# Moving the big on-chip tiles of a two-block transformer kernel to addresses that are multiples of 1024 bytes

## The chip, the cores and the metric

The kernel runs on one core of one Trainium2 chip. A core has a matmul engine (TensorE, PE in the profile; its weight loads are shown apart as PEld), VectorE (DVE), ScalarE (ACT), GpSimd (POOL) and SyncE (SP), which here issues nearly all DMAs. They share the on-chip memory SBUF, 128 partitions wide, in which a tile has one start address that is the same in all partitions. The metric is the device time of one execution in microseconds; lower is better.

## What is computed

The input is 256 tokens of 1024 features, float32, batch 1. Two transformer blocks of different kind follow each other:

```
x = first_block(x, mem, ...)          # one layer
#   h += [dilated attention | gated linear recurrence] @ w_out
#   h += cross attention to mem (q from h; k, v from rmsnorm(mem))
#   h += relu(rmsnorm(h) @ w_mlp_in)^2 @ w_mlp_out ; final rmsnorm
x = second_block(x, ...)              # two layers
#   z = rmsnorm(x) @ w_in ; MLA, FNet, differential attention, HGRN2 scan
#   x += (sum of gated branches) @ w_out
#   x += (silu(g) * u) @ w_down ,  [g | u] = rmsnorm(x) @ w_gate_up
```

All arithmetic is float32, and nearly all of the work is multiplying 256 tokens by some 190 MB of weights that are each used once.

## The kernel before

**Pieces.** The weights are packed on the host into 192 pieces of 128 partitions x 2048 floats (1 MB, 8192 bytes in a partition; 54 for the first block, 69 for each layer of the second). SyncE loads them in order into `ring`, a buffer of three pieces (`load_piece`, L993 to L1000).

**Split products.** A float32 matmul at full precision is replaced by three faster ones on split operands: w = w_hi + w_lo and x = x_hi + x_lo, and the product is x_hi w_hi + x_lo w_hi + x_hi w_lo. For each piece ScalarE writes `w_hi` (two instructions of 128x1024, L1125), VectorE writes `w_lo` = ring - w_hi (one of 128x2048, L1625), and TensorE then runs 48 matmuls of 256 columns (2 halves x 3 passes x 8 blocks of the contraction): `gemm` (L530 ff.), every one issued through `mm` (L508). `w_hi` and `w_lo` hold two pieces each, so that the next piece is split while TensorE works on this one. I call the 48 matmuls of a piece a job.

**Moving and stationary.** A matmul streams one operand (moving) past another that was loaded into the array before (stationary). In the "feat" form (L547) x moves and the weight is stationary: the profile names it `bank<-x_hi,w_hi`, moving operand first. In the "tok" form the weight moves and x is stationary: `bank<-w_hi,x_hi`. The product of the cross attention's keys and values uses `mem_hi` and `mem_lo` in the place of x. In the three down projections the weight moves in runs of 512 columns against the stationary hidden activations (`bank<-w_hi,hid_hi`). So a 256-column matmul reads 1024 contiguous bytes in each partition as moving operand and 512 bytes as stationary operand, whose place within a row of 1024 bytes is the operand's start (first half) or 512 bytes further (second half).

**Where tiles lie.** `sb` (L162) gives out SBUF in the order of the calls, L168 to L187. Four large tiles, `hid_hi`, `hid_lo`, `mem_hi` and `mem_lo`, are placed at offsets inside the arena `W` (L180 to L184), from which all scratch tensors are cut by number. Nothing in the program's order depends on addresses: steps, waits and semaphores are the same whatever they are.

The start addresses in the built program, and what is left after dividing by 1024:

| tile | before: address (mod 1024) | changed: address (mod 1024) |
|---|---|---|
| ring | 16512 (128) | 17408 (0) |
| w_hi | 41088 (128) | 41984 (0) |
| w_lo | 57472 (128) | 58368 (0) |
| const | 73856 (128) | 203808 (32) |
| vec | 85408 (416) | 215360 (320) |
| row | 85952 (960) | 215904 (864) |
| h | 94144 (960) | 74752 (0) |
| xs | 102336 (960) | 82944 (0) |
| x_hi | 110528 (960) | 91136 (0) |
| x_lo | 118720 (960) | 99328 (0) |
| oT | 126912 (960) | 107520 (0) |
| W (arena), hid_hi | 135104 (960) | 115712 (0) |
| hid_lo | 167872 (960) | 148480 (0) |
| mem_lo | 180160 (960) | 160768 (0) |
| mem_hi | 192512 (0) | 173120 (64) |
| junk | 223200 (992) | 224096 (864) |
| stat | 225248 (992) | 226144 (864) |
| rrow | 227296 (992) | 228192 (864) |

All sizes of one step inside these tiles (a block of 256 floats, a piece) are multiples of 1024 bytes, so what holds for the start holds for every block. Within the arena a few tensors have odd lengths, and what lies behind them stands 16 bytes further.

Of the kernel before, what the change touches and what calls it, by code (L numbers as in the profile page):

```python
# [37 lines left out]
P = 128  # L38
# [32 lines left out]
C_SIZE = C_MASK + len(MASKED) * P  # L71
# [12 lines left out]
V_SIZE = V_ZG + 2 * L2  # L84
# [6 lines left out]
R_SIZE = R_LAYER + L2 * R_PER  # L91
# [68 lines left out]
def build(nc, x_d, mem_d, xt_d, memt_d, pos_d, const_d, vec_d, row_d, rgw_d, pieces_d, out_d):  # L160
    with ExitStack() as ctx:
        def sb(name, shape, dt=F32):  # L162
            return ctx.enter_context(nc.sbuf_tensor(name, shape, dt))

        def sem(name):
            return ctx.enter_context(nc.semaphore(name))

        ring = sb("ring", [P, RING, PIECE])  # L168
        w_hi = sb("w_hi", [P, SPLITS, PIECE], F32R)
        w_lo = sb("w_lo", [P, SPLITS, PIECE], F32R)  # L170
        const = sb("const", [P, C_SIZE])
        vec = sb("vec", [P, V_SIZE])
        row = sb("row", [P, R_SIZE])
        h = sb("h", [P, TT, D])
        xs = sb("xs", [P, TT, D])
        x_hi = sb("x_hi", [P, KT, S], F32R)
# [5 lines left out]
        hid_lo = nc.alloc_sbuf_tensor_at("hid_lo", [P, 32, S], F32R, offset=arena0 + 4 * A_HID_LO)  # L182
        mem_hi = nc.alloc_sbuf_tensor_at("mem_hi", [P, KT, S], F32R, offset=arena0 + 4 * A_RGW)
        mem_lo = nc.alloc_sbuf_tensor_at("mem_lo", [P, KT, S], F32R, offset=arena0 + 4 * A_U)  # L184
        junk = sb("junk", [P, D], BF16)
        stat = sb("stat", [P, 512])
        rrow = sb("rrow", [P, S])  # L187
# [2117 lines left out]
```

## Time and profile before

| | us |
|---|---|
| median of 3 runs | 1295.13 (1294.65 to 1295.71) |
| the profiled execution | 1295.53 |
| its span, first to last instruction | 1293.7 |
| PE busy | 1265.9 (98%) |
| DVE busy | 862.2 (67%) |
| ACT busy | 652.5 (50%) |
| POOL busy | 114.4 (9%) |

The span is the stretch that the trace covers; 1.8 us of the profiled execution lie outside it. Busy PE is modelled from pipelined matmuls and says that PE almost never stands, not that it runs at its peak. How fast it runs is seen from the distance between the starts of successive matmuls.

### The profile page before, as it was taken

What the parts mean: (1) busy time and instruction counts of PE and PEld (TensorE: products, weight loads), DVE (VectorE), ACT (ScalarE), POOL (GpSimd) and SP (SyncE); (2) the same over time, 40 slices, a digit from 0 to 9 for tenths busy, and PEclk for the clock granted to TensorE, in tenths of its full rate; (3) what the DMA queues carried; (4) which work ended last, traced back from release to release, by engine and by line L of the source; (5) the groups of instructions that cost most, each with busy time, mean ns of one, the idle gap of its engine ahead of it and who ended that gap; (6) DMA issues with size and microseconds to landing.
All of it is one profiled execution on the core that took longest, in us unless ns stands there. A gap on an engine that the chain in (4) does not pass through costs nothing.

```text
span 1293.7 us, 22072 instructions
## 1 busy us (share of the span) xinstructions
PE 1265.9 (98%) x9208; PEld 1178.1 (91%) x9208; DVE 862.2 (67%) x1194; ACT 652.5 (50%) x1049; POOL 114.4 (9%) x152
## 2 busy tenths in 40 slices
PE   8999999999999999998999999999999999999998
PEld 8998999988788989997999998888899988999986
DVE  6897667644466675998656553667577996655543
ACT  5896655543368464342544443556552434544432
POOL 1100000000000000661000000000003810000000
PEclk8999999999999999999999999999999999999999
DMA  9543445555535323442555555433343325455552
GB/s 368 204 163 115 180 135 192 196 185 180 188 101 193 131 99 131 164 152 84 189 189 176 190 196 185 165 139 136 112 145 131 134 96 196 165 191 174 187 196 98
DMA packets 30324, 211.77 MB, mean 164 GB/s; under 512 B 3344, under 2 KB 3728, under 8 KB 5264
## 3 DMA queue, kind: packets, MB, share of 16 engines
q1 hardware_dynamic: 29936, 210.22, 45.5%
q8 instruction: 73, 1.20, 0.4%
q14 instruction: 27, 0.22, 0.1%
q10 hardware_dynamic: 288, 0.14, 0.0%
HBM read 209.29 MB, written 1.05 MB: 163 GB/s over the span
## 4 chain that ended last, share of the span: by engine, by line
PE 74%; DVE 13%; ACT 6%; issue 5%; DMA 1%; SPq 0%; DVEq 0%; ACTq 0%
PE bank L508 72%; DVE w_lo L1625 3%; ACT w_hi L1125 2%; DVE W L1599 2%; DMA ring<-weight_pieces 1%; ACT W L1125 1%; PE bank L608 1%; PE bank L843 1%; DVE xs L2125 1%; DVE W L1585 1%; DVE junk L2123 1%; DVE W L2105 1%; DVE W L1586 1%; DVE W L1617 0%; DVE stat L1558 0%
## 5 line engine op out<-in xcount | busy, mean ns | idle before, releaser
L1625 DVE TENSOR_TENSOR w_lo<-ring,w_hi 128x2048 fp32r<-128x2048 f32 x183 | 422.5, 2309 | 283.9 <-ACT w_hi L1125 283.5
L1125 ACT ACTIVATE w_hi<-ring 128x1024 fp32r<-128x1024 f32 (+1 forms) x368 | 366.2, 1046 | 241.9 <-PE bank L508 226.2
L508 PE MATMUL bank<-x_hi,w_hi 128*128 128x256 f32 x1840 | 267.2, 284 | 2.4 <-ACT w_hi L1125 2.4
L508 PE MATMUL bank<-x_hi,w_lo 128*128 128x256 f32 x1840 | 261.5, 281 | 1.0 <-DVE w_lo L1625 0.9
L508 PE MATMUL bank<-x_lo,w_hi 128*128 128x256 f32 x1840 | 254.8, 280 | 0.0
L508 PEld LDWEIGHTS bank<-x_hi,w_hi 128*128 128x128 f32 x1840 | 237.0, 189 | 5.7 <-issue 2.4
L508 PEld LDWEIGHTS bank<-x_hi,w_lo 128*128 128x128 f32 x1840 | 236.5, 188 | 2.3 <-DVE w_lo L1625 1.7
L508 PEld LDWEIGHTS bank<-x_lo,w_hi 128*128 128x128 f32 x1840 | 233.6, 188 | 0.0
L508 PE MATMUL bank<-W 128*128 128x128 f32 (+4 forms) x716 | 110.7, 327 | 8.3 <-ACT W L1125 4.8
L508 PEld LDWEIGHTS bank<-W 128*128 128x128 f32 (+3 forms) x716 | 87.8, 187 | 21.5 <-issue 12.3
L508 PE MATMUL bank<-w_lo,hid_hi 128*128 128x512 f32 x304 | 78.5, 394 | 0.0
L508 PE MATMUL bank<-w_hi,hid_hi 128*128 128x512 f32 x304 | 78.5, 394 | 0.0
L508 PE MATMUL bank<-w_hi,hid_lo 128*128 128x512 f32 x304 | 78.5, 394 | 0.0
L1104 POOL MEMSET W<- 128x512 f32 x32 | 16.8, 526 | 670.4 <-PE bank L508 667.3
L508 PEld LDWEIGHTS bank<-w_lo,hid_hi 128*128 128x128 f32 x304 | 56.8, 187 | 14.1
L508 PEld LDWEIGHTS bank<-w_hi,hid_lo 128*128 128x128 f32 x304 | 56.8, 187 | 14.1
L508 PEld LDWEIGHTS bank<-w_hi,hid_hi 128*128 128x128 f32 x304 | 56.6, 187 | 13.8
L508 PE MATMUL bank<-w_hi,x_hi 128*128 128x256 f32 (+1 forms) x400 | 64.8, 294 | 2.7 <-ACT x_hi L1125 2.7
L508 PE MATMUL bank<-oT,ring 128*128 128x256 f32 x256 | 57.7, 382 | 5.5 <-ACT oT L1125 2.7
L508 PE MATMUL bank<-w_lo,x_hi 128*128 128x256 f32 (+1 forms) x400 | 61.4, 284 | 1.1 <-DVE w_lo L1625 1.0
L508 PEld LDWEIGHTS bank<-oT,ring 128*128 128x128 f32 x256 | 47.8, 190 | 14.1 <-DVE W L2105 4.3
L508 PEld LDWEIGHTS bank<-w_hi,x_hi 128*128 128x128 f32 x400 | 54.1, 194 | 5.1 <-ACT x_hi L1125 3.1
(257 smaller groups left out, 1238.0 us busy)
## 6 DMA issues: line engine op xcount, KB each, us to landing
ring<-weight_pieces SPq DMA_DIRECT2D x191, 1024.0 KB, 4.8
const<-constants SPq DMA_DIRECT2D x1, 1376.5 KB, 8.9
W<-x_features SPq DMA_DIRECT2D x4, 256.0 KB, 5.2
ring<-weight_pieces SPq DMA_DIRECT2D x2, 512.0 KB, 6.0
h<-x SPq DMA_DIRECT2D x2, 512.0 KB, 11.9
W<-rg_weights SPq DMA_DIRECT2D x1, 1024.0 KB, 9.7
xs<-mem_features SPq DMA_DIRECT2D x1, 1024.0 KB, 11.4
oT<-mem SPq DMA_DIRECT2D x1, 1024.0 KB, 11.4
```

The lines of the kernel that those rows point to most:

```text
L508: return nc.tensor.matmul(out, lhsT, rhs, start=first, stop=last)
L608: ins = nc.tensor.transpose(bank[0:piece.shape[1], jj * S + tt * P:jj * S + (tt + 1) * P], piece, ident)
L843: ins = nc.tensor.transpose(bank[:, kt * S + qt * P:kt * S + (qt + 1) * P], prob[:, qt, kt * P:(kt + 1) * P], ident)
L1104: link(nc.gpsimd.memset(k, 0.0))
L1125: return nc.scalar.activation(out, in_, ACT.Copy, scale=scale)
L1585: v.tensor_tensor(x[:, :, :, 0, :], mid, f5[:, :, :, 0, :], ALU.subtract)
L1586: v.tensor_tensor(x[:, :, :, 1, :], f5[:, :, :, 1, :], mid, ALU.subtract).then_inc(s_decay_log, 1)
L1599: v.tensor_tensor(at(A_QL + 512 * (idx % 4), 2 * S), q, at(A_X + 512 * (idx % 4), 2 * S), ALU.mult).then_inc(s_query, 1)
L1625: v.tensor_tensor(w_lo[:, q % SPLITS, 0:n], raw(pp)[:, 0:n], w_hi[:, q % SPLITS, 0:n].bitcast(F32), ALU.subtract).then_inc(s_weight_low, 1)
L2105: drains(v.tensor_tensor(at(A_GATE, 16, S)[:, k:k + 2, :], bank2(wait_filled(dve, job)), rrow[:, None, :].broadcast_to([P, 2, S]), ALU.mul ...
L2123: drains(v.scalar_tensor_tensor(tmp, gk, 1.0, bank, ALU.add, ALU.mult), job)
L2125: ins = v.tensor_tensor(mk, mk, tmp, ALU.add)
```

## The change

A pad of 218 floats (872 bytes) is allocated first, and the three tables of constants (`const`, `vec`, `row`) are allocated behind the arena and the four tiles inside it, in place of ahead of `h`. No instruction is added, removed or reordered: engine by engine the instructions and their waits are the same, only their addresses differ. The address table above shows all that changes.

```
+        sb("to_1024_bytes", [P, 218])
         ring = sb("ring", [P, RING, PIECE])
         w_hi = sb("w_hi", [P, SPLITS, PIECE], F32R)
         w_lo = sb("w_lo", [P, SPLITS, PIECE], F32R)
-        const = sb("const", [P, C_SIZE])
-        vec = sb("vec", [P, V_SIZE])
-        row = sb("row", [P, R_SIZE])
         h = sb("h", [P, TT, D])
         xs = sb("xs", [P, TT, D])
         x_hi = sb("x_hi", [P, KT, S], F32R)
...
         mem_lo = nc.alloc_sbuf_tensor_at("mem_lo", [P, KT, S], F32R, offset=arena0 + 4 * A_U)
+        const = sb("const", [P, C_SIZE])
+        vec = sb("vec", [P, V_SIZE])
+        row = sb("row", [P, R_SIZE])
         junk = sb("junk", [P, D], BF16)
```

## Rows read from the trace of the kernel before

**Rows 1.** The page: span, busy shares, granted clock and chain.
```profile
span 1293.7 us, 22072 instructions
...
PE 1265.9 (98%) x9208; PEld 1178.1 (91%) x9208; DVE 862.2 (67%) x1194; ACT 652.5 (50%) x1049; POOL 114.4 (9%) x152
...
PEclk8999999999999999999999999999999999999999
...
PE 74%; DVE 13%; ACT 6%; issue 5%; DMA 1%; SPq 0%; DVEq 0%; ACTq 0%
```

**Rows 2.** Who waited for whom, whole span: total us, times, longest us.
```profile
DVE w_lo L1625 <- ACT w_hi L1125: 283.5, 143, 5.4
ACT w_hi L1125 <- PE bank L508: 226.2, 74, 7.1
```

**Rows 3.** Groups by shape, whole span: count, busy us, mean ns, idle before.
```profile
L508 PE MATMUL bank<-x_hi,w_hi 128*128 128x256 f32 x1840 | 267.2, 284 | 2.4 <-ACT w_hi L1125 2.4
...
L508 PE MATMUL bank<-w_hi,hid_hi 128*128 128x512 f32 x304 | 78.5, 394 | 0.0
...
L508 PE MATMUL bank<-w_hi,x_hi 128*128 128x256 f32 x384 | 58.2, 289 | 2.7 <-ACT x_hi L1125 2.7
```

**Rows 4.** Stretches: length, PE, PEld, DVE, ACT, POOL busy (count), clock, DMA share, GB/s.
```profile
111.00:132.00 21.00, 21.00 (x186) 20.98 (x186) 13.07 (x10) 11.17 (x22) 0.00 (x0) 1.00 0.48 178
...
660.00:760.00 100.00, 100.00 (x851) 100.00 (x850) 57.47 (x46) 45.44 (x54) 0.00 (x0) 1.00 0.54 190
270.00:350.00 80.00, 80.00 (x344) 64.12 (x343) 34.06 (x16) 28.11 (x28) 0.00 (x0) 1.00 0.53 184
907.60:912.60 5.00, 5.00 (x47) 5.00 (x46) 0.99 (x1) 3.98 (x9) 0.00 (x0) 1.00 0.04 13
```

**Rows 5.** Timeline of PE in one layer, 399.8 to 403.5: start, us, what, count.
```profile
401.67 1.07 PE L508 MATMUL bank<-w_hi,x_hi 128*128 128x256 f32 x8
402.58 1.07 PE L508 MATMUL bank<-w_hi,x_lo 128*128 128x256 f32 x8
```

**Rows 6.** Timeline of PE at the same place of the next layer, 866.6 to 870.4.
```profile
868.50 1.11 PE L508 MATMUL bank<-w_hi,x_hi 128*128 128x256 f32 x8
869.45 1.10 PE L508 MATMUL bank<-w_hi,x_lo 128*128 128x256 f32 x8
```

**Rows 7.** Timeline of PE, 81.5 to 89.3: products with the memory moving.
```profile
81.56 1.11 PE L508 MATMUL bank<-mem_hi,w_hi 128*128 128x256 f32 x8
82.50 1.11 PE L508 MATMUL bank<-mem_lo,w_hi 128*128 128x256 f32 x8
...
89.11 0.40 PE L508 MATMUL bank<-mem_hi,w_lo 128*128 128x256 f32 x2
```

**Rows 8.** Timeline of PE, 97.5 to 102.8: products with the memory stationary.
```profile
99.85 1.11 PE L508 MATMUL bank<-w_hi,mem_hi 128*128 128x256 f32 x8
100.80 1.07 PE L508 MATMUL bank<-w_hi,mem_lo 128*128 128x256 f32 x8
101.72 1.10 PE L508 MATMUL bank<-w_lo,mem_hi 128*128 128x256 f32 x8
```

**Rows 9.** Groups by shape, DVE and ACT, 512 floats in a partition.
```profile
L1631 DVE TENSOR_TENSOR hid_lo<-W,hid_hi 128x512 fp32r<-128x512 f32 x38 | 25.9, 682 | 0.0
...
L2105 DVE TENSOR_TENSOR W<-bank,rrow 128x512 f32<-128x512 f32 x32 | 21.9, 683 | 4.1 <-PE bank L508 3.9
L1512 ACT ACTIVATE W<-W 128x512 f32<-128x512 f32 x32 | 20.3, 633 | 72.0 <-DVE W L1586 71.4
L1171 ACT ACTIVATE W<-W 128x512 f32<-128x512 f32 x32 | 20.0, 624 | 12.6 <-DVE W L2105 12.6
```

**Rows 10.** The chain in order of time, its pieces that are DMAs: start, us.
```profile
3.35 6.83 DMA ring<-weight_pieces
...
503.48 4.81 DMA ring<-weight_pieces
...
970.26 4.75 DMA ring<-weight_pieces
```

**Rows 11.** DMA issues: count, KB each, median us from issue to landing.
```profile
ring<-weight_pieces SPq DMA_DIRECT2D x191, 1024.0 KB, 4.8
```

More of the change, by code:

```diff
@@ L166, in sem @@
             return ctx.enter_context(nc.semaphore(name))
+        sb("to_1024_bytes", [P, 218])
         ring = sb("ring", [P, RING, PIECE])
@@ L170, in build @@
         w_lo = sb("w_lo", [P, SPLITS, PIECE], F32R)
-        const = sb("const", [P, C_SIZE])
-        vec = sb("vec", [P, V_SIZE])
-        row = sb("row", [P, R_SIZE])
         h = sb("h", [P, TT, D])
@@ L184, in build @@
         mem_lo = nc.alloc_sbuf_tensor_at("mem_lo", [P, KT, S], F32R, offset=arena0 + 4 * A_U)
+        const = sb("const", [P, C_SIZE])
+        vec = sb("vec", [P, V_SIZE])
+        row = sb("row", [P, R_SIZE])
         junk = sb("junk", [P, D], BF16)
```

## The prediction

> **What bounds the kernel now.** I read the page first [rows 1]. PE is busy for 98% of the span, its granted clock is at the upper level (2.4 GHz) except for the first slices and short dips, and the chain that ended last is 74% PE, 13% DVE, 6% ACT and 1% DMA. Then the waits [rows 2]: the large ones are DVE waiting for ACT's half of a weight split, and ACT waiting for PE to give a split buffer free. Those engines stand because PE is slow, so they have slack. In 660 to 760 us, deep in a gate-up projection, PE is busy without a break while DVE is busy 57.47 of 100 us, ACT 45.44, and the DMA engines 0.54 [rows 4]. So the time is the number of matmuls times the distance from one start to the next, plus the stretches of attention and scan, where DVE and ACT lead.
>
> The distance is what an address could touch, and it is not in the groups, whose means (284 ns for a 256-column matmul, 394 ns for one of 512 [rows 3]) are durations of overlapping instructions. I take it from counts. In 660 to 760 us 851 matmuls touch the stretch, so some 851 starts in 100 us: 117.5 ns [rows 4]. In 111 to 132 us, where w moves and x is stationary, 186 in 21.00 us: 112.9 ns. In 270 to 350 us 344 matmuls of 512 columns in 80 us: 232.6 ns, or 116.3 for each 256 columns. The granted clock is 1.00 in all three, and PE never stands. A 256-column read at 2.4 GHz, one column a cycle, takes 106.7 ns, so PE loses some 11 ns of each 117.5, and there are two levels of that loss: an upper distance near 117.5 and a lower one near 113.
>
> **The change, part by part.** No instruction is added or moved, so every term is a count times a change of duration.
>
> *DVE, ACT and POOL: 0.* The trace before holds operations of one size at different alignments. DVE on 512 floats takes 682 ns where all three operands lie at 960 mod 1024 (hid_lo<-W,hid_hi) and 683 where one is `rrow`, at 992, only 32 bytes past a multiple of 64 [rows 9]. ACT takes 624 on tensors at 960 (L1171) and 633 on tensors behind the odd-length one, 16 bytes off (L1512). The 9 ns there are between different functions, and even if they were all alignment they would be worth 0.5 us if taken off some 50 such operations, under the cover of the slack above: ACT waits 226.2 us for PE in all [rows 2]. If that cover were gone, which happens only where DVE and ACT lead (19% of the chain [rows 1]), a change of 1% in their durations would be 1293.7 x 0.19 x 0.01 = 2.5 us; the rows give no reason for it.
>
> *DMA: 0, at most 1 us either way.* The ring moves from 128 mod 256 to a multiple of 256. A piece lands 4.8 us after its issue [rows 11] and a job lasts 48 x 117.5 ns = 5.64 us, so nearly all loads hide under PE. Three stand on the chain: 6.83, 4.81 and 4.75 us, 16.4 us together [rows 10]. No row has the same load at another alignment; I bound it at 5% of the 16.4 us on either side, 0.8 us, and take 0, since 4.75 and 4.81 lie within 0.05 of the median of all 191.
> The Trainium skill (DMA: Bandwidth & Descriptors, "How a descriptor splits into AXI transactions") says that a DMA transaction must start at a multiple of 256 bytes, so that a misaligned descriptor needs one more. By it 8192 bytes at 128 mod 256 cost 33 transactions and not 32, an estimate of 3% or 0.5 us on the 16.4. No row here shows it.
>
> *TensorE's distance: 0 where it is at the upper level.* The upper level already stands at several pairs of alignment. x moving from 960 against w at 128 and at 640 (the two halves of each job) gives 117.5 over 660 to 760 us, with both halves in it [rows 4]. `mem_hi` starts at a multiple of 1024 before the change. In the key products it moves against w: two passes of 8 with `mem_hi` and one with `mem_lo` (at 960) in turn. From 81.56 to 89.11 us lie 64 starts, 7.55 us, 118.0 ns, and its own first pass takes 0.94 us for 8, 117.5 [rows 7]. So a moving operand at a multiple of 1024 costs what one at 960 costs, within 0.5 ns. What no row holds is a pair with both operands at multiples of 512. I take 0, and the bounds from the levels: 112.9 below, and above, the slowest run of eight that I found, `w_hi` moving against `mem_hi` stationary at 512: 0.95 us for 8, 118.8 ns [rows 8].
>
> *TensorE's distance where it is at the lower level: up to +3 us.* The lower level occurs where w moves (128) and x is stationary (960 or 448): all four jobs of 111 to 132 us, down to the last such job at 907.60 to 912.60, 47 in 5.00 us [rows 4]. Going through the timeline job by job, I find it in 14 of the 24 w-moving jobs with x and in half of a 15th. It isn't fixed by the addresses: at the same place in two layers, with the same buffers and after the same wait, PE resumes at 0.91 us for eight (113.8 ns) in one [rows 5] and at 0.95 (118.8) in the other [rows 6]. But the addresses seem to permit or forbid it: with w moving against `mem_lo` at 448 eight take 0.92 us (115.0), and directly ahead of that against `mem_hi` at 512 0.95 us [rows 8]. The changed kernel puts x where `mem_hi` is here. If the lower level is lost altogether: 14.5 jobs x 48 x 4.6 ns (117.5 - 112.9) = 3.2 us. I count a quarter, +0.8 us, since a few of these jobs stand where PE waits anyway, and since the level is not bound to the address alone.
>
> The sum: 1295.53 + 0 + 0 + 0.8 = 1296.3 us against the profiled execution's own time. That execution lies 0.4 us above the median of the runs, 1295.13, so I forecast 1295.9. A measurement of this kernel can tell about 0.2%, 2.6 us, from no change; +0.8 lies within it.
>
> How little is needed to leave it: the matmuls that split products make are 3 x 1840 with x moving, 3 x 384 with w moving and 3 x 304 of 512 columns [rows 3], in units of 256 columns 5520 + 1152 + 1824 = 8496. 2.6 us over 8496 is 0.31 ns of 117.5.
>
> **The rivals.**
> *A. The lower level spreads (faster).* If x moving from a multiple of 1024 can fall to 112.9 like w moving from 128, PE gains 4.6 ns on 5520 matmuls: 25.4 us, and about 1270. If the down projections follow in proportion, 1824 x 3.4 = 6.2 us more: about 1264. DVE, ACT and DMA would allow it: 48 x 112.9 is 5.42 us a piece against 4.8 us for its load. For it: the lower level is seen with a moving operand at a multiple of 128, and x (960, 64 past one) never shows it in a long stretch. Against it: `mem_hi` moving from a multiple of 1024 stayed at 118.0, and w moving from 128 against the hidden activations stayed at 116.3. A part of it, in some jobs only, gives 3 to 25 us.
> *B. All of PE's loss goes (faster).* Without the loss the distance is 106.7 ns, and 8496 x 10.8 us/1000 = 92 us is the most that could come back, before the loads at 4.8 us a piece become the bound at 100 ns a matmul. Nothing in the rows comes near 107 at 256 columns.
> The Trainium skill (TensorE: Matmul & The Clock Gate, "Back-to-back issue gap") gives N / 2.4 + 2.5 ns between isolated matmuls, 109.2 for 256 columns. The trace does not agree: 117.5 in long streams, 112.9 at best. By the page the gain would be an estimate of 8496 x 8.3 ns = 71 us.
> *C. The two reads meet (slower).* After the change the moving and the stationary operand of every large product start at equal places mod 512. The place where before they both lie at multiples of 128 is the one with `mem_hi` stationary: 118.8 ns against 115.0 for its neighbour [rows 8]. If all products go to 118.8: (118.8 - 117.5) x 5520 = 7.2 us, w moving, whose mean I put at 115, 3.8 x 1152 = 4.4 us, and 1.3 x 1824 = 2.4 us for the down projections: +14 us, 1309. With only the w-moving jobs affected +3.2 to +4.4 us, 1298.3 to 1299.5. It decides from 0.31 ns a matmul. Against the full form: [rows 7] show no such price with `mem_hi` moving, and both halves of the x-moving jobs cost the same though their stationary places differ by 512 bytes.
> *D. Nothing at all.* The distances are set by something that doesn't see these address bits: 1295.1, within the same band as my forecast.
>
> **How the numbers follow.** Forecast and D together, within 0.2%: 0.44. A in full 0.10, A in part 0.16, B 0.01: faster 0.27. C with the w-moving jobs alone 0.17, spread further 0.12: slower 0.29. The range leaves out A in full and most of a deep A (about 0.13) and C beyond half of its full price (about 0.06): 1283 to 1303. The likeliest case's own range is 1294.2 to 1297.7.
>
> **What the profile of the changed kernel would show.** If I am right: 850 or so matmuls in a 100 us stretch of gate-up, 344 in 80 us of the down projection, DVE and ACT group means for 512 floats within 2 ns of 682 and 624, and the landing of a piece still at 4.8 us. A loss of the lower level shows as 178 or 179 matmuls in 21 us of the first block's output projection, not 186. A shows as 885 in 100 us. C shows as 842. If the time moves by more than 0.2% with all of these unchanged, the cause is in attention and scan, on DVE or ACT, and my zero for them is wrong. What would make the prediction wrong is any shift of the long x-moving streams, since they are 65% of the units.

## The result and the profile after

The changed kernel takes 1301.8 us (median of 4, 1300.29 to 1302.03) against 1295.42 us for the kernel before in the same session: ratio 1.0046, 95% interval [1.0029, 1.0064]. It is slower by about 0.5%: the interval leaves out 1, and the time lies inside the stated range. The profiled execution took 1300.29 us with a span of 1298.5, 4.8 us over the span before [rows 1]; it is the fastest of the four, so its span shows less of the loss than the medians do (6.4 us). Two executions of the experiments below came out at a low mean clock (1376.63 us at 0.849 for the pad alone, 5062.78 us at 0.236 with x 128 bytes past w) and are left out of every ratio; the first is the only trace of the pad alone, so no distances are read for it.

The page of the changed kernel, the parts that answer to [rows 1]:

```profile
span 1298.5 us, 22072 instructions
...
PE 1271.8 (98%) x9208; PEld 1191.8 (92%) x9208; DVE 862.3 (66%) x1194; ACT 652.5 (50%) x1049; POOL 114.5 (9%) x152
...
PE 79%; DVE 11%; issue 5%; ACT 4%; DMA 1%; DVEq 0%; ACTq 0%
```

DVE, ACT and POOL are busy for as long as before to within 0.1 us. PE is busy for 5.9 us more and has a larger share of the chain, 79% against 74%. The waits that answer to [rows 2], in the changed kernel:

```profile
DVE w_lo L1626 <- ACT w_hi L1126: 278.6, 145, 5.4
...
ACT w_hi L1126 <- PE bank L509: 224.6, 74, 7.1
```

The groups of 512 floats on DVE and ACT (compare [rows 9]):

```profile
L1632 DVE TENSOR_TENSOR hid_lo<-W,hid_hi 128x512 fp32r<-128x512 f32 x38 | 25.9, 681 | 0.0
L2106 DVE TENSOR_TENSOR W<-bank,rrow 128x512 f32<-128x512 f32 x32 | 21.9, 683 | 4.5 <-PE bank L509 4.4
L1513 ACT ACTIVATE W<-W 128x512 f32<-128x512 f32 x32 | 20.2, 632 | 71.5 <-DVE W L1587 70.9
L1172 ACT ACTIVATE W<-W 128x512 f32<-128x512 f32 x32 | 20.0, 624 | 12.4 <-DVE W L2106 12.4
```

They changed by at most 1 ns. The DMA row that answers to [rows 11]:

```profile
ring<-weight_pieces SPq DMA_DIRECT2D x191, 1024.0 KB, 4.8
```

What moved is the distance between matmuls. The stretches of [rows 4] in the changed kernel (length, then PE, PEld, DVE, ACT, POOL busy with counts, clock, DMA share, GB/s):

```profile
111.00:132.00 21.00, 21.00 (x175) 20.85 (x174) 11.99 (x10) 11.29 (x23) 0.00 (x0) 1.00 0.46 162
270.00:350.00 80.00, 80.00 (x355) 66.23 (x354) 36.30 (x18) 30.55 (x32) 0.00 (x0) 1.00 0.56 196
660.00:760.00 100.00, 100.00 (x835) 100.00 (x835) 58.16 (x44) 42.97 (x51) 0.00 (x0) 1.00 0.52 183
```

Compare the counts, at an equal clock of 1.00. x moving: 835 in 100 us and not 851, 119.8 ns and not 117.5. w moving in the first output projection: 175 in 21 us and not 186, 120.0 and not 112.9. The down projection, in runs of 512 columns: 355 in 80 us and not 344, 225.4 and not 232.6. So two parts lose and one wins. In a timeline of PE at the place of [rows 5]:

```profile
402.54 1.12 PE L509 MATMUL bank<-w_hi,x_hi 128*128 128x256 f32 x8
403.50 1.12 PE L509 MATMUL bank<-w_hi,x_lo 128*128 128x256 f32 x8
```

eight matmuls take 0.96 us, against 0.91 in the one layer and 0.95 in the other before [rows 5, 6].

For exact means I took, from each trace, the distances between the starts of successive matmuls of one kind, without those that contain a wait (over 0.52 ns a column, 133 ns for 256 columns). Before: x moving 117.8, w moving against x 115.2, down projection 233.3. After: 119.9, 119.9 and 226.8. By counts, 5520 x 2.1 + 1152 x 4.6 - 912 x 6.5 = 11.6 + 5.3 - 5.9 = +11.0 us.

The span grew by 4.8 only. Both traces hold the same 9208 matmuls in the same order, so the time from each start to the one before can be summed by kind, waits included:

| kind | before, us | after, us | change | by distance alone |
|---|---|---|---|---|
| x moving | 662.6 | 672.2 | +9.6 | +11.6 |
| w moving against x, 256 columns | 142.0 | 144.6 | +2.6 | +5.3 |
| down projections | 212.5 | 206.5 | -6.0 | -5.9 |
| all other matmuls | 271.2 | 269.8 | -1.4 | |

So some 6 us of the 11.0 are missing, nearly all in shorter waits. Where DVE or ACT lead, a slower PE uses up time in which it would have stood. About 1 us of it is the start: the same matmul that starts at 25.8 us in the trace before starts 0.7 us earlier in this one, and over the first 17 us the granted clock was 0.80 in that trace and 0.90 in this. The down projections have no such waits, so their gain came through whole: first to last hidden start, the three take 212.1 us before and 206.1 after.

### The profile page after: what moved, and what is told of

Read it like the earlier page. It is cut to its first block, busy times and chain, and to the rows that moved or that the text cites. A ratio compares the mean times of both kernels' runs of the same rounds, so it can differ in the third digit from the quotient of the medians.

```text
span 1298.5 us, 22072 instructions
## 1 busy us (share of the span) xinstructions
PE 1271.8 (98%) x9208; PEld 1191.8 (92%) x9208; DVE 862.3 (66%) x1194; ACT 652.5 (50%) x1049; POOL 114.5 (9%) x152
## 4 chain that ended last, share of the span: by engine, by line
PE 79%; DVE 11%; issue 5%; ACT 4%; DMA 1%; DVEq 0%; ACTq 0%
PE bank L509 77%; DVE w_lo L1626 2%; DVE W L1600 2%; ACT w_hi L1126 2%; PE bank L609 1%; PE bank L844 1%; DVE xs L2126 1%; ACT W L1126 1%; DVE W L1586 1%; DVE junk L2124 1%; DVE W L2106 1%; DMA ring<-weight_pieces 1%; DVE W L1587 1%; DVE W L1618 0%; ACT W L1375 0%
## 5 line engine op out<-in xcount | busy, mean ns | idle before, releaser
L509 PE MATMUL bank<-x_hi,w_hi 128*128 128x256 f32 x1840 | 270.2, 286 | 3.1 <-ACT w_hi L1126 3.1
L509 PE MATMUL bank<-x_hi,w_lo 128*128 128x256 f32 x1840 | 264.8, 283 | 0.7 <-DVE w_lo L1710 0.3
L509 PE MATMUL bank<-x_lo,w_hi 128*128 128x256 f32 x1840 | 258.8, 283 | 0.0
L509 PEld LDWEIGHTS bank<-x_hi,w_hi 128*128 128x128 f32 x1840 | 240.2, 192 | 6.4 <-issue 2.9
L509 PEld LDWEIGHTS bank<-x_hi,w_lo 128*128 128x128 f32 x1840 | 240.5, 192 | 1.7 <-DVE w_lo L1626 1.2
L509 PEld LDWEIGHTS bank<-x_lo,w_hi 128*128 128x128 f32 x1840 | 237.7, 192 | 0.0
## 6 DMA issues: line engine op xcount, KB each, us to landing
h<-x SPq DMA_DIRECT2D x2, 512.0 KB, 11.6
oT<-mem SPq DMA_DIRECT2D x1, 1024.0 KB, 11.6
```

Of the source, the lines that this page charges most:

```text
L509: return nc.tensor.matmul(out, lhsT, rhs, start=first, stop=last)
```

## The experiments

Theory R was formed on the two traces: the distance is set, for each product apart, by the start of the moving operand minus that of the stationary one, modulo a small power of two. Its rivals: A, it is set by where the moving operand itself lies; S, by the whole layout. Below, "difference" is moving minus stationary mod 256. In the kernel before it is 64 for x moving against w, 192 for w against x and for w against the hidden activations; in the changed kernel it is 0 for all three. From run to run only addresses differ. Times are medians, with the ratio to the kernel before of the same session.

**Both with an equal shift: the pad alone.**

```
+        sb("to_1024_bytes", [P, 218])
         ring = sb("ring", [P, RING, PIECE])
```

> Only the pad of 872 bytes is added to the kernel before; the tables stay ahead of h. Ring, w_hi and w_lo come to 0 mod 1024, x, oT and the arena to 832. The difference x minus w, 832 (320 mod 512), is that of the kernel before. Theory R (the distance between matmuls is set by the difference of the moving and the stationary operand's start, mod 512): all as before, 1295.4 us, x moving 117.5 ns, w moving against x down to 113 in part of the jobs, down projection 233 ns. Theory A (it is set by the moving operand's own place in a row of 1024 bytes): w moves from 0 now as in the changed kernel, so w moving 120 and the down projection 226, x moving (832, a multiple of 64 and not of 128, as 960 was) 117.5 as before; 5.5 us lost and 6.8 us won, 1294 us.

1294.23 us against 1294.52, ratio 0.9998 [0.9988, 1.0009]. Ring and split weights stand at multiples of 1024 and nothing happens. R holds for the time; A expected 1294 too, so the time alone doesn't part them.

**The tables moved, without the pad: 128 for all.**

```
-        const = sb("const", [P, C_SIZE])   # these three behind the arena, as in the change
-        vec = sb("vec", [P, V_SIZE])
-        row = sb("row", [P, R_SIZE])
```

> The changed kernel without its pad: all the large tiles at 128 mod 1024, the difference x minus w 0. Theory R: as the changed kernel, x and w moving 120 ns, down projection 226, 1301.8 us. Theory A: nothing stands at a multiple of 1024; w moves from 128 as in the kernel before (113 to 117.5, down projection 233), and x now too: 1295 us or less, to 1270 if x takes the lower level.

1301.79 us, ratio 1.0053 [1.0038, 1.0068]: the changed kernel's time with no large tile at a multiple of 1024. Its stretches:

```profile
270.00:350.00 80.00, 80.00 (x357) 66.30 (x356) 35.16 (x18) 31.11 (x32) 0.00 (x0) 1.00 0.56 197
660.00:760.00 100.00, 100.00 (x836) 100.00 (x835) 58.28 (x44) 44.21 (x53) 0.00 (x0) 1.00 0.54 189
```

836 and 357, as in the changed kernel. A falls here: w moves from 128, as before the change, and the distances are those after it. The multiple of 1024 plays no part. Nor is it the place of the stationary operand alone: w, which is stationary when x moves, lies at 128 in this kernel, in the kernel before and in the next two, and x moving takes 119.9 ns here, 117.8 in the kernel before, 115.7 and 119.9 in those two. The ring is back at 128 mod 256 here, and the time is still that of the changed kernel.

**x 192 and 256 bytes past w.**

```
         w_lo = sb("w_lo", [P, SPLITS, PIECE], F32R)
+        sb("shift", [P, 48])               # 192 bytes; [P, 64] for 256; tables behind the arena, no pad
         h = sb("h", [P, TT, D])
```

> As the kernel without a pad, but with 192 bytes between w_lo and h, so that x minus w is 192 mod 512, the difference that w minus x had in the kernel before. Theory R: x moving takes the lower level of 113 ns that w moving had there, 4.5 ns less on 5520 matmuls, 25 us; w moving against x now has the difference 320 and stands at 117.5; the down projection too has 320 mod 512, which no run shows for it, 226 to 233. 1270 us, and not over 1280. Theory A: x at 320 mod 1024 (64 past a multiple of 128) as before 117.5, w as before: 1295 us.

1287.6 us, ratio 0.9936 [0.9914, 0.9957]. Faster, but by 6.9 us and not by the 25 that R said, and over its limit of 1280. x moving has a mean of 115.7 ns, not 113, since it takes the lower level in some stretches and the upper in others:

```profile
180.00:260.00 80.00, 80.00 (x682) 80.00 (x681) 54.73 (x69) 43.42 (x60) 0.00 (x0) 1.00 0.53 185
660.00:760.00 100.00, 100.00 (x850) 99.96 (x849) 57.93 (x44) 43.76 (x54) 0.00 (x0) 1.00 0.54 189
1120.00:1220.00 100.00, 100.00 (x885) 100.00 (x884) 59.13 (x47) 47.15 (x57) 0.00 (x0) 1.00 0.56 198
```

682 in 80 us (117.3) and 850 in 100 (117.6) beside 885 in 100 us (113.0); the last two are the same stage of two layers. w moving, now at 64, has 117.8, the level that x moving had at 64 before. The two have changed places, as R says.

> The same with 256 bytes: x minus w is 256 mod 512, and so is w minus x, so that all products have one difference, the one furthest from that of the changed kernel. Theory R: x moving and w moving alike, at one level; if the loss is a meeting of the two reads, this one is at or under 113 ns, 1265 to 1272 us; if 256 is as bad as 0, 120 ns and 1302. Theory A: x at 384, a multiple of 128 like w before: 113 to 117.5, 1270 to 1295 us, with the down projection at 233 as before.

1300.79 us, ratio 1.0049 [1.0032, 1.0065], x and w moving 119.9, the down projection 226.8. 256 is as 0: what counts is the difference modulo 256 (or a divisor of it). Only 0 and 256 were compared this way, for both widths; for the other differences the period is assumed.

**The arena back to difference 0, x at 192, 128, 160 and 224.** Each gives two points, since x moving has d and w moving -d.

```
+        sb("shift", [P, 48])               # 192; 32, 40 or 56 floats for the others
...
+        sb("shift_back", [P, 16])          # so that both pads make 256 bytes
         W = sb("W", [P, ARENA])
```

> x 192 bytes past w as in the run before, and 64 bytes more between oT and the arena, so that the hidden activations come back to the difference 0 mod 256. Theory R (each product has its own distance, set by moving minus stationary mod 256): x moving (192) keeps its mean of 115.8 ns, w moving against x (64) 117.8, and the down projection falls from 230.2 to the 226.8 that it has at difference 0: 3.1 us under the 1287.6 of that run, 1284.5. Rival S (what counts is where x lies, or the whole layout, not the pair): the down projection stays at 230, 1287.6.

1286.53 us, ratio 0.9929 [0.9914, 0.9944], the lowest median of the study, though the intervals don't part it from the earlier run with x at 192 or from the winning half alone below. The down projection is at 226.8 (354 in 80 us), x moving at 115.6.

```profile
180.00:260.00 80.00, 80.00 (x708) 80.00 (x707) 55.77 (x69) 44.80 (x63) 0.00 (x0) 1.00 0.54 186
270.00:350.00 80.00, 80.00 (x354) 66.25 (x353) 33.59 (x16) 30.11 (x30) 0.00 (x0) 1.00 0.56 197
660.00:760.00 100.00, 100.00 (x840) 99.47 (x839) 57.47 (x45) 45.52 (x54) 0.00 (x0) 1.00 0.52 184
1120.00:1220.00 100.00, 100.00 (x851) 100.00 (x851) 57.45 (x46) 45.52 (x54) 0.00 (x0) 1.00 0.54 190
```

Now the stage at 180 us has the lower level (708 in 80 us, 113.0), which had the upper one two runs before, with x at 192 too, and the stage at 1120 us has the upper, where it had the lower. (The 840 at 660 us are the upper level too: the last 3 us of that stretch already belong to the down projection, whose matmuls are twice as wide.)

The trace also shows something that R doesn't foresee. w moving has the difference 64 here, at which it stayed at 117.8 two runs before, and x moving stayed at 117.8 in the kernel before. But two of its jobs, from 388 and from 853 us, run at 113.3 ns (mean over all 117.3). The lower level isn't bound to the difference 192. The down term is confirmed in the distances; the time fell by 1.1 us and not 3.1, which the run-to-run spread of this layout (1283.91 to 1287.28, and 1281.59 to 1289.09 for the earlier run with x at 192) covers, so in the time alone it is inconclusive.

> x 128 bytes past w, arena at difference 0. Both x moving and w moving have the difference 128 mod 256, as far from 0 as can be. If the loss is a meeting of the two reads that 0 makes worst, this is the best: 113 ns or less for both, 1265 to 1272 us. If the loss is periodic in 128 bytes, it is 119.9 for both as at 0, and 1302. By the products with mem_hi stationary in the kernel before (difference 128, 118.8 ns in runs of eight) 118 to 119, 1295 to 1299.

1297.32 us, ratio 1.0016 [1.0006, 1.0026]. x moving 118.8, w moving 118.7, against 119.9 at 0, inside the third of the expectations. Neither the best nor the same as at 0: the price isn't a meeting that grows as the difference shrinks, and it isn't periodic in 128. The products with mem_hi in the kernel before, whose difference is 128, had foretold this one: 118.8 in the run of eight that [rows 8] show.

> x 160 bytes past w: x moving has 160, w moving 96 mod 256, arena 0. Nothing measured at these. Theory R, read as a smooth function between the measured 192 (115.8) and the unknown 128: 113 to 119 for x moving, 1270 to 1300 us. If only the multiple of 64 counts (32 bytes more or less make no difference), x moving goes as at 128 or at 192.

1294.4 us, ratio 0.9996 [0.9987, 1.0005]. x moving (160) 117.9, w moving (96) 119.9. 96 is as slow as 0 (119.9), though 64 and 128 are faster than both.

> x 224 bytes past w: x moving has 224, w moving 32 mod 256, arena 0. Theory R as a smooth function between 192 (115.8) and 0 (119.9): 116 to 120 for x moving, w moving (32) between 117.8 and 119.9: 1285 to 1302 us. If the steps are of 64 bytes, as at 192 or as at 0.

1292.64 us, ratio 0.9985 [0.9975, 0.9994]. x moving (224) 118.3, w moving (32) 116.9. Outside my bounds for w moving: the curve isn't smooth between 0 (119.9) and 64 (117.8).

**The winning half alone.** The kernel before with 192 bytes between oT and the arena.

```
+        sb("shift", [P, 48])
         W = sb("W", [P, ARENA])
```

> The kernel before with 192 bytes between oT and the arena and nothing else: x keeps its difference to w (64 mod 256), the hidden activations come to the difference 0. Theory R: the down projections alone fall from 233.3 to 226.8 ns, 912 matmuls, 5.9 us; w and x moving against each other stay at 115.3 and 117.8: 1294.9 - 5.9 = 1289.0 us. This is the half of the change that wins, alone. Rival S (the whole layout): no part of the gain, 1294.9.

1287.21 us against 1295.9, ratio 0.9939 [0.9918, 0.996]. Its profiled execution has a span of 1288.3, 5.4 under that of before, where 5.9 was expected:

```profile
270.00:350.00 80.00, 80.00 (x354) 66.25 (x353) 33.93 (x16) 29.79 (x30) 0.00 (x0) 1.00 0.55 192
660.00:760.00 100.00, 100.00 (x851) 100.00 (x850) 57.72 (x43) 43.91 (x53) 0.00 (x0) 1.00 0.53 189
```

354 in 80 us for the down projection, and 851 in 100 us for x moving, as before. S falls. The medians lie 8.7 us apart, more than 5.9, but the interval (5 to 11 us) holds both. A small part of the excess may be the lower level, which x moving has in some jobs here at the difference 64 (mean over all 117.6), eight matmuls in 0.91 us:

```profile
640.02 1.07 PE L509 MATMUL bank<-x_hi,w_lo 128*128 128x256 f32 x8
640.93 1.07 PE L509 MATMUL bank<-x_hi,w_hi 128*128 128x256 f32 x8
```

**The down projection at 32, and x at 208.**

```
+        sb("shift_more", [P, 8])           # first: x at 192, arena 32 bytes further, at 224
...
+        x_hi = sb("x_hi", [P, KT * S + 64], F32R)[:, 4:KT * S + 4].rearrange(...)  # second; x_lo alike
```

> x 192 past w, arena 224 past w, so that the down projection (w moving minus hidden) has 32 mod 256, not tried before for 512 columns. At 0 it is 226.8 ns, at 64 230.2, at 192 233.3. Theory R as a smooth function: 227 to 230, 1285 to 1289 us; x moving about 115.7 as in the two runs with 192. If 32 is the better place for 512 columns as well as it was for w moving (116.9 against 119.9 at 0), under 226: 1284 us or less.

1289.73 us, ratio 0.9957 [0.994, 0.9974]. The down projection has 233.3 ns, outside both expectations: 32 is as bad as 192 for 512 columns, while it was good for 256. The best difference of one width isn't that of the other. And w moving, at the difference 64, has the lower level in three jobs (mean over all 117.1), eight matmuls again in 0.91 us:

```profile
855.21 1.07 PE L510 MATMUL bank<-w_hi,x_lo 128*128 128x256 f32 x8
856.12 1.07 PE L510 MATMUL bank<-w_lo,x_hi 128*128 128x256 f32 x8
```

> x_hi and x_lo start 208 past w mod 256 (16 bytes more than 192, as a slice of a longer tile), arena 0. At 192 x moving alternates between stretches of 113.3 and 117.8, at 224 it stays at 118.3. If the lower level belongs to a window of differences that 192 lies at the edge of, 208 is inside it and stays at 113: 1270 to 1275 us. If 192 is a point, 208 is like 224: 117 to 118.5, 1290 to 1293 us.

1295.8 us, ratio 1.0004 [0.9995, 1.0013]. x moving 119.1 throughout, slower than both expectations; w moving, at 48, has 116.7. No window around 192: the lower level is seen at 192 and, in a few jobs, at 64 (the same two addresses with the roles of moving and stationary exchanged), and at none of the other six multiples of 32, nor at 48 or 208.

**The losing half alone.** The changed kernel with the arena 64 bytes further.

```
         oT = sb("oT", [P, KT, S])
+        sb("shift", [P, 16])
         W = sb("W", [P, ARENA])
```

> The changed kernel with 64 bytes between oT and the arena: x and w keep the difference 0, the hidden activations go back to the difference that they had in the kernel before (w minus hidden 192 mod 256). This is the half of the change that loses, alone. Theory R: the down projections go back from 226.8 to 233.3 ns, 5.9 us over the changed kernel: 1307.7 us, about 12.5 us or 1.0% over the kernel before. Rival S (the whole layout, or being at multiples of 1024, makes the price): 1301.8 still, or back towards 1295 since the arena leaves its multiple of 1024.

1307.83 us against 1295.91, ratio 1.0099 [1.0079, 1.012], within 0.2 us of what R gave.

```profile
272.00:352.00 80.00, 80.00 (x344) 64.48 (x343) 34.18 (x18) 30.00 (x31) 0.00 (x0) 1.00 0.55 195
660.00:760.00 100.00, 100.00 (x836) 100.00 (x835) 57.55 (x45) 44.43 (x53) 0.00 (x0) 1.00 0.51 180
```

The first stretch starts 2 us later than in [rows 4], since the down projection starts later here; it holds 344 matmuls of 512 columns in 80 us, as many as before the change, and the mean over all three projections is 233.3 ns. x moving stays at 836 in 100 us. S falls again. So the change is the sum of two parts: +12 us with x and w at difference 0, -6 us with the hidden activations at difference 0.

All distances in one table, mean ns from start to start without waits. Each is from 900 to 5400 matmuls of one trace, but those marked * are from 46: one product of the first block (162 to 173 us before) moves w in runs of 512 columns against x, so that its difference follows x. It has 233.3 at 192 and at 32 as the down projections have, and 226.7 to 227.7 at 0 and 229.0 at 64, within 1.3 ns of them.

| difference mod 256 | 256 columns | 512 columns |
|---|---|---|
| 0 | 119.9 | 226.8 |
| 32 | 116.9 | 233.3 |
| 48 | 116.7 | 231.9* |
| 64 | 117.1 to 117.8, most jobs at 117.8, a few at 113.3 | 230.2 |
| 96 | 119.9 | 233.3* |
| 128 | 118.7 | 232.5* |
| 160 | 117.9 | |
| 192 | 115.2 to 115.8, mixed of 113.3 and 117.8 | 233.3 |
| 208 | 119.1 | |
| 224 | 118.3 | |

## Why the prediction was right or wrong

**What bounds the kernel, and that only PE's distance can move: right.** DVE and ACT groups stayed within 1 ns, and the differences are in the distances of matmul starts and the waits between them. Of the forecast's numbers, the likeliest case's own range (1294.2 to 1297.7) was missed; the wide one held.

**DMA, 0: right.** The ring came to a multiple of 256 and the landing is unchanged at 4.8 us; the pad alone made 0.9998, and without the pad, with the ring back at 128 mod 256, the time was the same (1301.79 us).
The Trainium skill's extra transaction for a misaligned descriptor (DMA: Bandwidth & Descriptors, "How a descriptor splits into AXI transactions"), 0.5 us by my estimate, is less than these runs can show; the section speaks of bytes that a transaction reads, and here it is the end that is written that moved.

**"TensorE's distance: 0 where it is at the upper level": the step that failed.** It rose by 2.1 ns on 5520 matmuls. I read the evidence by the place of one operand, where the difference of two counts. [rows 7] have mem_hi moving from a multiple of 1024, but against w at 128, which is the difference 128 and not the 0 that the change makes; that 118.0 and 117.5 lay near each other said nothing about 0. I had noted that no row holds the pair, and then took 0 from the neighbour. And 0.31 ns was all that was needed. The same zero stood for the down projections, which I had at 116.3 for each 256 columns beside the upper level: they changed by 6.5 ns on 912 matmuls, -5.9 us.

**The lower level of w moving: right in kind, too small.** It was lost altogether and not by a quarter, and the jobs went past the upper level to 119.9: 4.6 ns on 1152 matmuls, 5.3 us, in place of 0.8; shorter waits took up 2.7 of them.

**Rival C, the two reads meet: right in its direction, wrong in one term and in its ground.** I gave +1.3 ns for x moving (2.1 measured), 3.8 for w moving (4.6), and +2.4 us for the down projections, which won 5.9. Carrying a price per 256 columns over to 512 was the fault: the two widths have different best differences. Its 14 us, with these three put right (+4.4, +0.9 and -8.3) and 6.2 us of waits taken off, are the 4.8 us of the span. The ground was wrong too: the 118.8 came from `mem_hi`, at the difference 128, which isn't the one that the change makes, and 96 costs as much as 0, which a meeting of the two reads doesn't explain.

**That the range held is partly luck.** It reached to 1303 because C was in it up to half of its price. What kept the time under 1303 is a gain in the down projections and waits that took up 6 us, and the sum has neither. Without the gain the kernel takes 1307.83 us, outside the range.

**Rival A.** Its gain came true in part in another layout, but not under its condition: x lies there at 320 mod 1024, with the difference 192, took the lower level in about half of its matmuls, and the kernel took 1287.6.

**Open.** Nothing here shows what chooses between the lower level of 113.3 and the upper of 117.8. In the three traces with x at 192 the level never changes inside a stream of 16 or more such matmuls without a wait, also where the stream goes over from x moving to w moving; in the kernel before it changes at that very place with no wait between (at 393 and 860 us). If the lower level held throughout, x moving alone would give 5520 x 2.4 = 13 us more. Nor is it shown why a given difference costs what it costs; the runs establish the dependence, not its mechanism. While a matmul streams, the weight load of the next one overlaps it (PEld is busy for 1178.1 us beside PE's 1265.9 [rows 1]); as `w_hi` and `w_lo` are alike modulo 256, and `x_hi` and `x_lo` too, no run tells the matmul's own stationary operand from the next one's.

## What to carry to other kernels

An alignment isn't good by being round. If matmuls stream float32 operands back to back, look at the start-to-start distance of each product, and vary the start of the moving tile against the stationary one in steps of 32 bytes, for each width apart; a pad of 192 bytes was worth 0.6% here in a kernel whose PE was already busy for 98% of the span. A row at another alignment is evidence only if the quantity that counts is the same in it.

## What was not expected of the hardware

How fast matmuls follow each other depends on the address of the moving operand relative to the stationary one, modulo 256 bytes, by up to 6% (113.3 to 119.9 ns at 256 columns) and 3% (226.8 to 233.3 at 512), at a granted clock of 1.00.
The Trainium skill (SBUF — State Buffer, "Who interferes with whom") lists for PE two independent read ports, one for the moving operand and one for weight loads, and says that PE never waits on anyone. The distances here depend on the pair of addresses, so for these float32 operands, at 0.44 to 0.47 ns a column, the two reads don't come out as independent in their timing; the measurement decides.

The same layout can run a stage at 113.3 or at 117.8 ns throughout, and in another execution of nearly the same layout the other way round. That may be why its times spread more, which no trace of the single executions shows (1281.59 to 1289.09 us in five executions at the difference 192, against 1300.29 to 1302.03 in four at 0).
